# First mixer's units: where the state products, the output gates and the readouts stand

## The reference

```python
def hgrn2_mixer(h_lat, h_ctx, w_in, lb_fwd, lb_bwd, gnorm, w_out, slot, need_ctx):
    # w_in gives q, v, zf, zb, g; for each of 8 heads and 2 directions, in chunks of 64:
    #   scores = (q*exp(cum-ref)) (k*exp(ref-cum))^T, lower triangle;  intra = scores v
    #   chunk_kv = (k*exp(last-cum))^T v;  S <- exp(last) S + chunk_kv
    #   inter = (q*exp(cum)) S_prev;  o = intra + inter
    return readout(o_lf + rev(o_lb), gl, gnorm, w_out)   # need_ctx is False: y_ctx is not wanted

def _hgrn_readout(o, g, gnorm, w_out):
    o = o * lax.rsqrt(jnp.mean(o * o, axis=-1, keepdims=True) + EPS) * gnorm
    y = o * silu(g)                      # heads side by side, 1024 wide
    return y @ w_out
```

## Time and profile before

| | us |
|---|---|
| median of 3 runs | 2016.06 (2015.94 to 2017.7) |
| the profiled execution, its own time | 2016.28 |
| its span | 2015.0 |
| TensorE busy | 1953.8 (97%) |
| VectorE busy | 1322.0 (66%) |
| ScalarE busy | 1056.4 (52%) |
| granted TensorE clock, mean | 0.989 |

### The profile page before, as it was taken

How to read it: one execution, slowest core, us unless ns; L and a number is a source line. 1 busy time by engine, 2 the same in 40 slices (tenths; PEclk the granted TensorE clock), 3 DMA queues, 4 the chain that set the end, 5 groups by cost and what they waited for, 6 DMA issues and landing times.

```text
span 2015.0 us, 26351 instructions
## 1 busy us (share of the span) xinstructions
PE 1953.8 (97%) x10828; PEld 1649.5 (82%) x10828; DVE 1322.0 (66%) x1682; ACT 1056.4 (52%) x1337; POOL 7.3 (0%) x8
## 2 busy tenths in 40 slices
PE   9899989999999999999999999999999999999998
PEld 4788877778889888888887888897788898888886
DVE  3877665688875566665795665656665675567654
ACT  4337664577754456444564544455544454555443
POOL 0000000000000000000000000000000000000000
PEclk9999999999989999999998999999999999999999
DMA  9851216699955444655421555451356555346561
GB/s 346 294 173 59 84 43 227 235 324 312 308 183 166 149 145 163 203 183 196 139 84 63 188 175 202 154 185 64 128 188 207 173 189 183 126 147 207 171 207 73
DMA packets 230563, 354.86 MB, mean 176 GB/s; under 512 B 7690, under 2 KB 180523, under 8 KB 230188
## 3 DMA queue, kind: packets, MB, share of 16 engines
q1 hardware_dynamic: 229714, 352.90, 52.0%
q10 hardware_dynamic: 730, 0.27, 0.1%
HBM read 352.10 MB, written 1.05 MB: 175 GB/s over the span
## 4 chain that ended last, share of the span: by engine, by line
PE 87%; DVE 6%; ACT 4%; issue 1%; DMA 1%; POOL 0%; SPq 0%; DVEq 0%; ACTq 0%
PE bank L599 14%; PE bank L601 13%; PE bank L600 13%; PE bank L639 11%; PE bank L618 6%; PE bank L619 6%; PE bank L620 6%; PE bank L637 5%; PE bank L1212 2%; DVE wlo L1905 1%; ACT whi L1359 1%; PE bank L962 1%; DMA raw<-in_hg_w_in 1%; PE bank L642 1%; PE bank L730 1%
## 5 line engine op out<-in xcount | busy, mean ns | idle before, releaser
L1905 DVE TENSOR_TENSOR wlo<-raw,whi 128x2048 fp32r<-128x2048 f32 x282 | 644.3, 2290 | 219.2 <-ACT whi L1359 217.9
L1359 ACT CAST whi<-raw 128x2048 fp32r<-128x2048 f32 x282 | 536.1, 1907 | 156.5 <-PE bank L601 119.0
L639 PE MATMUL bank<-HH,whi 128*128 128x512 f32 x1024 | 365.7, 397 | 0.5
L599 PE MATMUL bank<-whi,YH 128*128 128x512 f32 x816 | 321.5, 394 | 6.4 <-DVE YL L2486 2.5
L618 PE MATMUL bank<-HH,whi 128*128 128x256 f32 (+1 forms) x1024 | 314.9, 307 | 10.8 <-ACT ARENA L1498 4.0
L600 PE MATMUL bank<-wlo,YH 128*128 128x512 f32 x816 | 319.4, 391 | 0.0
L601 PE MATMUL bank<-whi,YL 128*128 128x512 f32 x816 | 319.4, 391 | 0.0
L620 PE MATMUL bank<-HH,wlo 128*128 128x256 f32 (+1 forms) x1024 | 306.9, 300 | 0.0
L619 PE MATMUL bank<-HL,whi 128*128 128x256 f32 (+1 forms) x1024 | 306.9, 300 | 0.0
L637 PE MATMUL bank<-HH,wlo 128*128 128x256 f32 x896 | 252.2, 282 | 0.0
L639 PEld LDWEIGHTS bank<-HH,whi 128*128 128x128 f32 x1024 | 192.2, 188 | 44.5 <-issue 1.5
(11 more groups left out here) (383 smaller groups left out, 2180.6 us busy)
## 6 DMA issues: line engine op xcount, KB each, us to landing
raw<-in_ffn_w SPq DMA_DIRECT2D x128, 1024.0 KB, 5.3
raw<-in_ret_w_in SPq DMA_DIRECT2D x48, 1024.0 KB, 5.2
ARENA<-in_w_mod SPq DMA_DIRECT2D x21, 1024.0 KB, 9.9
raw<-in_hg_w_in SPq DMA_DIRECT2D x20, 1024.0 KB, 7.4
raw<-in_ret_w_out SPq DMA_DIRECT2D x16, 1024.0 KB, 4.9
raw<-in_moe_w_gate SPq DMA_DIRECT2D x26, 512.0 KB, 5.0
raw<-in_moe_w_up SPq DMA_DIRECT2D x26, 512.0 KB, 6.0
raw<-in_moe_w_down SPq DMA_DIRECT2D x12, 1024.0 KB, 7.2
```

Source lines behind the costliest of these rows:

```text
L599: pe.matmul(ps, lh, rh, start=start, stop=False)
L639: x = pe.matmul(bank[bs[m]][:, :], w[0][:, k, c], HW[:, k, :], start=k == 0, stop=k == 7, skip_group_check=True)
L1359: ac.copy(whi[i % NS][:, :], raw[place[i]][:, :]).then_inc(*whi_("w", i))
L1905: ve.tensor_tensor(wlo[i % NS][:, :], raw[place[i]][:, :], f32(whi[i % NS][:, :]), SUB).then_inc(*wlv("w", i))
```

## The change

TensorE: `proj_b` gets a parameter `between`, a function that it calls after its steps k = 0 and 1 (12 of 48 matmuls). `unit_state(u)` is passed as this function instead of standing ahead of the block: in the z block for units 0 to 5, in a gate block for units 6 and 7.

The output gates' blocks 0 and 1 stand in unit 6, block 2 in unit 7, block 3 after the units; before, block 0 stood in unit 4. `OUT_GATE` follows.

The readouts: `READ_OUT` is gone, and each step has a place of its own. Square 0 in unit 5, sums 0 in unit 6, spread 0 and sums 1 in unit 7, spread 1 and sums 2 after block 3, spread 2 and sums 3 after the first tile of the output product, spread 3 after the second. Sums and spreads take their bank from the ring. `HSQ` and `HSG` lie in `G2B` instead of `ARENA`, each with a wait for its last reader, and each pair has its own four columns `HRS[p]`. On VectorE `routing` stands in unit 6 instead of 7. The closing's other passages are kept.

```diff
--- before.py
+++ after.py
@@ -110,13 +110,11 @@
 
 
 
-
-OUT_GATE = (4, 6, 7, 7)
+OUT_GATE = (6, 6, 7, 7)
 
 
 MOD_FIRST = (0, 2, 1, 3)
 MOD_SUMS = ((), (4,), (5,), (6,), (7,), (8,), (9,))
-READ_OUT = {4: 0, 6: 1, 7: 2}
 
 
 def weights(I):
@@ -331,7 +329,7 @@
         SC = [ar(12800 + 512 * i, 512) for i in range(2)]
         kd2 = two(ar(13824, 512))
         DEC = SM[:, 144:160]
-        HSQ, HSG = ar(9216, 512), ar(9728, 512)
+        HSQ, HSG = G2B[:, 0:512], G2B[:, 512:1024]
 
         MRAW = [ar(o, 2048) for o in (10240, 6144, 8192, 12288)]
         MFIRST = [r[:, :] for r in raw[0:3]] + [ar(o, 2048) for o in (0, 10240, 6144, 8192, 4096)]
@@ -339,7 +337,7 @@
         MACC = [ar(14336, 512), G2B[:, 0:512]]
         raw += [ar(12688, 2048), ar(5632, 2048)]
         MLATE = [ar(o, 2048) for o in (4352, 6400, 10240, 12688)]
-        HRS = SM[:, 50:54]
+        HRS = [SM[:, 50 + 4 * p:54 + 4 * p] for p in range(4)]
 
 
 
@@ -600,12 +598,15 @@
                 pe.matmul(ps, lh, rl, start=False, stop=False)
                 return pe.matmul(ps, ll, rh, start=False, stop=stop)
 
-            def proj_b(use, acts=None, n=256, ready=None, group=RING):
+            def proj_b(use, acts=None, n=256, ready=None, group=RING, between=None):
+
 
                 a = acts or H8
                 bs = [banks.next(pe, group, "b", use, m) for m in range(n // 256)]
                 i, w = take()
                 for k in range(8):
+                    if k == 2 and between is not None:
+                        between()
                     if ready is not None and k % 2 == 0:
                         if k == 2 and ready in CLOSE:
                             turned(ready, 1)
@@ -821,9 +822,9 @@
                                       stop=d == 1 and h == 1 and n == 3, skip_group_check=True)
                 x.then_inc(*mm("out", u))
 
-            def sums(p, b):
-
-                banks.hold(pe, b, "hg_sums", p)
+            def sums(p):
+
+                b = banks.next(pe, RING, "hg_sums", p)
                 pe.wait_ge(*act.at("hg_sq", p))
                 for h in range(2):
                     for t in range(2):
@@ -831,14 +832,14 @@
                                       ones[:, 0:1], start=True, stop=True)
                 x.then_inc(*mm("hg_sums", p))
 
-            def spread(p, b):
-
-                banks.hold(pe, b, "hg_spread", p)
+            def spread(p):
+
+                b = banks.next(pe, RING, "hg_spread", p)
                 pe.wait_ge(*vec.at("hg_scales", p))
                 for h in range(2):
                     for t in range(2):
                         n = 2 * h + t
-                        x = pe.matmul(bank[b][:, 128 * n:128 * n + 128], HRS[:, n:n + 1].to_broadcast([128, 128]), ident,
+                        x = pe.matmul(bank[b][:, 128 * n:128 * n + 128], HRS[p][:, n:n + 1].to_broadcast([128, 128]), ident,
                                       start=True, stop=True)
                 x.then_inc(*mm("hg_spread", p))
 
@@ -903,27 +904,31 @@
                 for n in MOD_SUMS[6]:
                     mod_sums(n)
                 for u in range(8):
-                    p = READ_OUT.get(u)
                     unit_scores(u)
-                    unit_state(u)
-                    if u == 6:
+                    state_of = lambda: unit_state(u)
+                    if u < 6:
+                        proj_b(("z", u + 2), H16, 512, between=state_of)
+                    elif u == 6:
                         shifts()
-                    if u < 6:
-                        proj_b(("z", u + 2), H16, 512)
-                    if p is not None:
-                        sums(p, 1)
-                        proj_b(("g", p), H16)
+                        proj_b(("g", 0), H16, between=state_of)
+                        sums(0)
+                        proj_b(("g", 1), H16)
+                    else:
+                        spread(0)
+                        proj_b(("g", 2), H16, between=state_of)
+                        sums(1)
                     unit_out(u)
-                    if p is not None:
-                        spread(p, 2)
                 proj_b(("g", 3), H16)
+                spread(1)
+                sums(2)
                 for j in range(4):
                     pe.wait_ge(*vlo.at("hg_y", j))
                     proj_a("hg", Y8, 2 * j, j == 0, j == 3)
                     if j == 0:
-                        sums(3, 4)
+                        spread(2)
+                        sums(3)
                     if j == 1:
-                        spread(3, 5)
+                        spread(3)
 
             def moe():
                 def mod_late(count):
@@ -1511,17 +1516,21 @@
 
                 def squares(p):
                     ac.wait_ge(*vps.at("hg_out", p))
+                    if p:
+                        ac.wait_ge(*mm.at("hg_sums", p - 1))
                     ac.activation(HSQ, QO[:, 2 * p:2 * p + 2, :], ACT.Square).then_inc(*act("hg_sq", p))
 
                 def silu_gate(p):
                     b = banks.of("b", ("g", p), 0)
                     ac.wait_ge(*prj.at("b", ("g", p)))
+                    if p:
+                        ac.wait_ge(*vec.at("hg_gated", p - 1))
                     ac.activation(HSG, bank[b][:, :], ACT.Silu).then_inc(*aps("g", p))
                     banks.free(("b", ("g", p), 0), aps)
 
                 def scales(p):
                     ac.wait_ge(*vec.at("hg_mean", p))
-                    ac.activation(HRS, HRS, ACT.Sqrt).then_inc(*act("hg_scales", p))
+                    ac.activation(HRS[p], HRS[p], ACT.Sqrt).then_inc(*act("hg_scales", p))
 
                 def high(p):
                     s = slice(2 * p, 2 * p + 2)
@@ -1529,29 +1538,34 @@
                     ac.copy(Y8[0][:, s, :], QO[:, s, :]).then_inc(*ahi("hg_y", p))
 
                 for u in range(8):
-                    p = READ_OUT.get(u)
                     ac.wait_ge(*trn.at("kdt", u, 0))
                     b = banks.of("kdt", u, 0)
                     ac.copy(KDT[:, 0, :, :], bank[b][:, :]).then_inc(*aps("kdt", u))
                     banks.free(("kdt", u, 0), aps)
                     if u < 7:
                         unit_gate(u + 1)
-                    if p is not None:
-                        ac.wait_ge(*mm.at("state", u))
-                        squares(p)
-                    if u < 7:
                         unit_vec(u + 1)
-                    if u < 6:
                         take()
-                    if p is not None:
+                    if u == 5:
+                        squares(0)
+                    if u == 6:
+                        silu_gate(0)
+                        scales(0)
                         take()
-                        silu_gate(p)
-                        scales(p)
-                        high(p)
+                        squares(1)
+                high(0)
+                take()
+                silu_gate(1)
+                take()
+                squares(2)
+                scales(1)
+                silu_gate(2)
+                high(1)
+                scales(2)
                 take()
                 squares(3)
                 silu_gate(3)
-                take()
+                high(2)
                 scales(3)
                 take()
                 high(3)
@@ -2254,7 +2268,7 @@
                 def mean(p):
                     b = banks.of("hg_sums", p)
                     ve.wait_ge(*mm.at("hg_sums", p))
-                    ve.tensor_scalar(HRS, bank[b][:, 0:4], 1.0 / 128, EPS, MUL, ADD).then_inc(*vec("hg_mean", p))
+                    ve.tensor_scalar(HRS[p], bank[b][:, 0:4], 1.0 / 128, EPS, MUL, ADD).then_inc(*vec("hg_mean", p))
                     banks.free(("hg_sums", p), vec)
 
                 def gated(p):
@@ -2264,7 +2278,7 @@
 
                 def scales(p):
                     ve.wait_ge(*act.at("hg_scales", p))
-                    ve.reciprocal(HRS, HRS).then_inc(*vec("hg_scales", p))
+                    ve.reciprocal(HRS[p], HRS[p]).then_inc(*vec("hg_scales", p))
 
                 def scaled(p):
                     y, b = slice(2 * p, 2 * p + 2), banks.of("hg_spread", p)
@@ -2281,30 +2295,36 @@
                     banks.free(("hg_out", p), vps)
 
                 for u in range(8):
-                    p = READ_OUT.get(u)
                     unit_scores(u)
+                    if u == 7:
+                        scaled(0)
                     unit_state(u)
                     if u < 7:
                         unit_vec(u + 1)
-                    else:
-                        routing()
-                    if p is not None:
-                        mean(p)
-                    if u < 6:
+                        if u == 6:
+                            routing()
                         take()
-                    if p is not None:
+                    if u == 6:
+                        mean(0)
+                        scales(0)
+                        gated(0)
                         take()
```

(15 more changed lines are left out.)

## The result

| | before | changed kernel |
|---|---|---|
| median (lowest to highest), us | 2016.48 (2015.94 to 2017.85), 5 runs | 2005.12 (2004.68 to 2009.99), 5 runs |
| the profiled execution, its span | 2016.28, 2015.0 | 2005.12, 2003.8 |
| granted clock, mean | 0.989 | 0.989 |

The ratio is 0.9949, 95% interval 0.9938 to 0.996: faster by 11.4 us, where 15.1 were forecast. 2005.12 lies just above the forecast range of 1998.8 to 2005.0.

What follows compares the result with a forecast made beforehand. TensorE, busy 97% of the span, was taken as the bound, so its waits are kernel time. 9.7 - 0.8 + 4.4 + 3.0 - 0.8 - 0.4 = 15.1 us off the 2016.06 median gave 2001.0, range 1998.8 to 2005.0.

Steps and rivals of the forecast that it cites:

- Part 1: State products between k=1 and k=2 of the projection cover the keys' copy: 9.7 us gained, 0.8 lost entering blocks twice.
- parts 2 and 3: Later readouts, squares ahead: pauses before sums go, 4.4 us, low clock 3.0; places made late cost 0.8 and 0.4.
- unit 7's wait: TensorE before unit 7's state products: VectorE needs 20.9 us, TensorE 20.1, so a wait of about 0.8 us.
- the sums 3 wait: TensorE before pair 3's sums, whose ring bank silu_gate(3) frees: 8.4 us against 8.0, a wait of about 0.4.
- No weights are missing: Projection blocks in the units: weights are split three tiles ahead of use, and no row names that as TensorE's releaser.
- the clock falls at a wait that is left: Rival: low clock behind a remaining wait, as before unit 7's products; 1.3 to 1.5 us each, 2002.4 to 2004; chance 0.12.
- The forecast's 3.0 us for the low clock before the sums: Gate blocks behind the readout pauses in units 6 and 7 return to full clock, 2.7 us, plus 0.25 at the sums.
- Behind this stage nothing gives it back: From 338 to 560 us TensorE waits for no weights; its largest wait there is 1.8 us in three pieces.
- These loads move with TensorE: SyncE's late modulation weights and third expert tile, loaded after the last sums, keep pace with TensorE; bound 0 to 2 us.
- VectorE's pace: Rival: VectorE's loop, 16.6 of 17.7 us, sets the units' pace; 3 to 7 us lost, priced 2006; chance 0.10.
- a loss in the experts: Rival: DMA transfers set the expert tiles' pace, so coming earlier gains nothing: 2016 us, same; chance 0.04.
- The serial closing: Rival: closing readouts run in series through single buffers and in-order queues, costing 23.4 us: 2024, slower; chance 0.04.

Runs made afterwards that it cites:

- Experiment 7: Kernel before with state products moved into the blocks in units 0 to 5 alone, sums 9 in bank 0, gate block 0 in bank 3: 2009.54 us, ratio 0.9966.
- experiment 5: Changed kernel with the state products ahead of the block again in all eight units, readouts and gates as changed: 2010.74 us, ratio 0.9968.
- experiment 8: Changed kernel with modulation sums 9 in bank 0 and the third expert tile loaded ahead of SyncE's wait: 1999.48 us, ratio 0.991.
- experiment 2: Changed kernel with modulation sums 9 in bank 0 instead of a ring bank: 2001.52 us, ratio 0.992.
- Experiment 3: Changed kernel, but in unit 0 alone the state products stand ahead of the gate block, as before: 2001.21 us, ratio 0.9919.
- experiment 1: Changed kernel run again with no edit: 2004.32 us, ratio 0.9927 to the kernel before.
- experiment 6: Kernel before with state products moved into the blocks in units 0 to 5 alone, gates and readouts as before: 2017.24 us, ratio 1.0005.
- 9: Changed kernel, but SyncE loads the second expert tile only after the root of pair 2: 2003.27 us, ratio 0.9941.
- Experiment 4: Changed kernel with the third expert tile loaded ahead of SyncE's wait for sums 3 and the late modulation weights: 2001.23 us, ratio 0.9916.
- experiment 10: Changed kernel, but SyncE also waits for the root of pair 3 before loading constants and late modulation weights: 2004.1 us, ratio 0.994.

## Why the prediction was right, and where not

**Direction and mechanism: right.** Part 1 hides the keys' copy, parts 2 and 3 take the pauses before the sums and the low clock. Experiment 7 gives 6.8 us of stage time for the one (in units 0 to 5), experiment 5 7.5 for the others. Both together, banks mended (experiment 8), end the output product at 320.36 with scores from 146.51 on: 173.85 us instead of 190.62, so 16.8. That is 2.5 more than 6.8 + 7.5: 1.5 is the fall of the clock in experiment 5's execution, and 1.0 is left for units 6 and 7, on which part 1 acts only in experiment 8. The forecast of the stage was 15.1. What it held too dear: unit 7's wait, 0.37 instead of 0.8, and the sums 3 wait, which isn't there, instead of 0.4 (its two sums are off by 0.1 each: their terms make 8.3 and 8.1, a wait of 0.2). The 0.9 left is not split further. The 0.05 us for a slower first product behind a pause stood on no row; the eight products took 1.13 us behind one and 1.05 without. The period came as forecast, 17.6 to 17.7 for 17.7, and VectorE stayed beside it.

**The failed step: the block that part 1 moves up was checked for its weights alone ("No weights are missing").** For each moved step I asked which data it waits for, and for the new users of the ring whether they get a bank ("the ring's banks for sums and spreads cost nothing" came true: no wait stands at them). I did not ask which bank the block itself needs, once it starts 3 us earlier. In unit 0 this is a pause of 2.68 us, and 2.95 us of the stage (176.80 to 173.85, experiment 8; 2.97 in experiment 2), of which the forecast held none. Experiment 3 shows the same cover from the other side. The trace of the kernel before had it. ScalarE frees the bank at 151.59 + 0.59 = 152.18, the block starts at 152.68: half a microsecond of cover, for a block that was to start at 149.4. Its rows:

```profile
151.59 0.59 ACT L1425 ACTIVATE ARENA<-bank 128x512 f32<-128x512 f32 x1
```
```profile
152.68 0.50 PE L618 MATMUL bank<-HH,whi 128*128 128x512 f32 x1
```

With this step 16.8 becomes the 13.8 of the trace.

**The clock behind it.** The rival "the clock falls at a wait that is left" was put at another place and a price of 1.3 to 1.5. The fall is real, but a matter of the execution: 1.6 us in experiment 1, nothing in the profile after. The forecast's 3.0 us for the low clock before the sums are of this kind too: behind unit 7's pause of 2.1 us the clock fell in the kernel before and in experiment 6, and stayed at 1.00 in experiment 7.

"Behind this stage nothing gives it back" was wrong by 2.6 us in this trace: 1.4 before the router (below) and 1.2 later, where the clock is the largest single piece. Both kernels pause 1.78 us at the same products, near 1370 us before and 1356 in the changed kernel; of these two traces only the changed one has a low clock behind it, 2.9 us. The first fence is the changed kernel, the second the kernel before, same work:

```profile
1345.00:1365.00 20.00, 18.22 (x118) 16.47 (x119) 10.21 (x20) 10.73 (x16) 0.00 (x0) 0.83 0.23 63
```
```profile
1359.00:1379.00 20.00, 18.22 (x147) 16.76 (x148) 10.55 (x21) 11.98 (x18) 0.00 (x0) 1.00 0.22 66
```

The repeat (experiment 1) has it at the same pause, 0.83 again, so it takes the other kernels to tell that it is no cost of the new order: experiments 2, 8 and 9 have that order and no low clock behind this pause, and experiment 6, with the old readouts, has one. What decides it is open. Over all runs the changed kernel lay between 2000.9 and 2010.0, and a range of 6 us for a single figure should have had room for it.

**"These loads move with TensorE", bound 0 to 2 us.** They moved with sums 3, as said, but not fully: 1.4 us came back before the router (0.79 to 2.16), inside the bound though taken at 0. Experiment 4 shows the place, the third expert tile behind the wait; for the cause of its late landing experiment 10 speaks for the table load, with the open ends said there.

**The account.** 15.1 forecast; +1.7 for the better units and closing; -2.95 for the bank; -1.4 before the router; -1.2 between 560 us and the end, where clock and small pauses differ in both directions and the -2.9 near 1356 stands against +1.7 before it: 11.2.

**The rivals.** VectorE's pace and a loss in the experts did not come: between the router and 560 us the lead stayed 12.4. The serial closing did not come either: sums 3 wait for nothing, and gate block to output product run without a pause. Of the Trainium skill's two rules, the one on the entry, read as a second entry that is free, is not borne out: the first record is 0.47 us in unit 2 and the next 0.40 or 0.39, as in the earlier trace rows. The one on the clock ("TensorE: Matmul & The Clock Gate", on psum-queue depth-cycling) is borne out only by single falls, not by an oscillation at every group. Experiment 5 has one in its unit 6 (0.69 from 265 to 270 us), some 4.5 us behind a pause of 0.83 us and behind 16 small products; no run separates the two. The kernel before has both in the same order (the pause at 270.89) and no fall until the sums, and behind the seven other pauses of 0.83 us in experiment 5 the clock stayed at 1.00. The two waits that part 3 left did not bring a low stretch, as the rival took from the rule: unit 7's, 0.37 us, has 1.00 behind it, and the other isn't there.

## What to carry to other kernels

When a block of matmuls is moved up, ask not only for its operands but for the PSUM bank that it takes at its start: who reads that bank last, when, and what covered that wait in the old order. A step that is moved often hid two waits, and a ring of banks shifts for everybody when one user is added or taken out (experiment 6). A wait of the loading queue on a late step should hold back only the loads that need it.

## What the runs showed of the hardware

- The clock behind a pause of one length is not fixed. Behind 2.68 us in unit 0 it stayed at 1.00 in three executions (the changed kernel, experiments 4 and 10) and fell to about 0.6 in three others (1, 6 and 9). Behind 2.1 us in unit 7 it fell in two (the kernel before, experiment 6) and not in a third (7). The price of a pause is its length plus the chance of a fall, and the falls priced here cost 1.3 to 2.9 us each.
- SyncE's issue of the first modulation tile took 0.97 to 1.56 us in the six executions in which it began beside ScalarE's table load and no tile was on its way, and 0.43 or 0.44 in the four in which it stood clear of it; its 1 MB landed 6.6 to 7.7 us after the start of the issue, against 5.4 to 5.8. With an expert tile issued just ahead (experiments 4 and 8) the first issue took 0.43 us beside the table load too, so the table load alone doesn't make an issue slow.
- A releaser named "issue" in the profile can be a bank of PSUM: experiment 2 removed such a wait by a bank alone.
